# A 32-expert layer in a two-block transformer kernel: experts in a computed order, a fourth weight place, bias sums inside the first slots

## What is computed

```python
logits = xt @ w_router + b_router                       # 512 x 32
top_vals, top_idx = lax.top_k(logits, 4)
gates = softmax(top_vals)
# every token goes to its 4 experts; for the rows xb of expert e:
gt = minimum(xb @ w_gate[e] + b_gate[e], 7)
up = clip(xb @ w_up[e] + b_up[e], -7, 7)
hid = gt * sigmoid(1.702 * gt) * (up + 1)
y = hid @ w_down[e] + b_down[e]
out = sum over the 4 choices of gate * y
x = layer_norm(ALPHA * h + out)
```

## Time and profile before

| | us |
|---|---|
| median of 3 runs | 2679.3 (2677.22 to 2679.68) |
| profiled execution | 2679.23 |
| its span | 2677.5 |
| TensorE matmul busy | 2380.6 (89%) |
| VectorE busy | 644.8 (24%) |
| ScalarE busy | 321.6 (12%) |
| DMA | 570.64 MB, mean 213 GB/s |

### The profile page before, as it was taken

The page is one execution under the profiler, slowest core; times in us unless marked ns, Lnnn a source line. Parts: engine busy times, 40 slices in busy tenths (PEclk is TensorE's granted clock), DMA queues, the critical chain, the costliest instruction groups (busy, mean ns, idle before and its releaser), DMA issues. The chain is left out here.

```text
span 2677.5 us, 25039 instructions
## 1 busy us (share of the span) xinstructions
PE 2380.6 (89%) x9489; PEld 1036.1 (39%) x9490; DVE 644.8 (24%) x1376; ACT 321.6 (12%) x653; POOL 306.4 (11%) x295
## 2 busy tenths in 40 slices
PE   6999999798999999898978878999999889998980
PEld 4445666443444444344453223333333223332320
DVE  1322556441000000413343111111111111111116
ACT  1211222300000000003110000111111001110100
POOL 1003111002110010201210000000000000000005
PEclk7999999799999999899967988999999889998995
DMA  7353222202512122220045999889968999989954
GB/s 301 157 188 80 79 87 95 87 0 96 230 63 82 44 94 79 77 100 1 8 186 202 418 420 407 307 297 361 361 233 339 420 420 368 372 316 421 356 200 173
DMA packets 189003, 570.64 MB, mean 213 GB/s; under 512 B 12279, under 2 KB 47276, under 8 KB 186892
## 3 DMA queue, kind: packets, MB, share of 16 engines
q1 hardware_dynamic: 172832, 528.15, 51.4%
q0 software_dynamic: 6432, 21.66, 2.2%
q10 hardware_dynamic: 9676, 19.99, 2.2%
HBM read 545.57 MB, written 24.18 MB: 213 GB/s over the span
## 5 line engine op out<-in xcount | busy, mean ns | idle before, releaser
L1997 PE MATMUL banks<-expert_ring,slot_xT_gate 128*64 128x512 f32 x1440 | 370.6, 662 | 102.4 <-DMA expert_ring<-in_w_gate_dram 101.8
L1997 PE MATMUL banks<-expert_ring,hiddenT 128*64 128x512 f32 x1440 | 318.4, 595 | 2.1 <-DVE hiddenT L2067 2.1
L1997 PE MATMUL banks<-expert_ring,slot_xT_up 128*64 128x512 f32 x1440 | 318.9, 595 | 0.0
L1997 PEld LDWEIGHTS banks<-expert_ring,slot_xT_gate 128*64 128x64 f32 x1440 | 110.8, 152 | 324.0 <-issue 306.8
L1168 PE MATMUL banks<-hT,weight_ring 128*128 128x512 f32 x512 | 223.5, 597 | 6.7 <-PEq L2186 4.6
L1186 PE MATMUL banks<-weight_ring,hidden_T 128*128 128x512 f32 x512 | 220.7, 593 | 1.6 <-PE banks L1168 1.2
L1997 PEld LDWEIGHTS banks<-expert_ring,hiddenT 128*64 128x64 f32 x1440 | 103.6, 138 | 208.8 <-issue 206.4
L1997 PEld LDWEIGHTS banks<-expert_ring,slot_xT_up 128*64 128x64 f32 x1440 | 99.4, 137 | 187.4 <-issue 187.4
L2060 DVE TENSOR_TENSOR up_act_T<-banks,expert_bias_T 128x512 f32<-128x512 f32 x45 | 31.1, 692 | 503.9 <-PE banks L1961 503.9
L1168 PEld LDWEIGHTS banks<-hT,weight_ring 128*128 128x128 f32 x512 | 97.4, 192 | 132.4 <-issue 132.4
L1186 PEld LDWEIGHTS banks<-weight_ring,hidden_T 128*128 128x128 f32 x512 | 96.9, 190 | 125.3 <-issue 125.3
(11 more groups left out here) (372 smaller groups left out, 2190.4 us busy)
## 6 DMA issues: line engine op xcount, KB each, us to landing
expert_ring<-in_w_gate_dram SPq DMA_DIRECT2D x128, 1024.0 KB, 12.3
expert_ring<-in_w_up_dram SPq DMA_DIRECT2D x128, 1024.0 KB, 17.7
expert_ring<-in_w_down_dram SPq DMA_DIRECT2D x128, 1024.0 KB, 8.7
weight_ring<-in_w_ada_dram SPq DMA_DIRECT2D x12, 2048.0 KB, 11.3
weight_ring<-in_w_in_dram SPq DMA_DIRECT2D x8, 2048.0 KB, 14.7
weight_ring<-in_w_ff_in_dram SPq DMA_DIRECT2D x8, 2048.0 KB, 8.5
weight_ring<-in_w_ff_out_dram SPq DMA_DIRECT2D x8, 2048.0 KB, 7.8
weight_ring<-in_w_in_dram SPq DMA_DIRECT2D x24, 512.0 KB, 6.6
```

The costliest lines, as they stand in the source:

```text
L1997: x = nc.tensor.matmul(ps[h * CAP:(h + 1) * CAP, bank, :], lhs[:, k % 4, (k // 4) * CAP:(k // 4 + 1) * CAP], X.ring[:, m, k, h * HALF:(h + ...
```

## The change

- **An order of the experts.** The place of an expert is computed on the chip. Its key is 32 times its slots minus its number; experts 0 and 1 get the two lowest keys (0 and -1), so their ranks are 30 and 31. `place` lists the rank that stands at each place: 30, 31, then 0, 10, 20, 1, 11, 21, ... 9, 19, 29. So experts 0 and 1 come first, then one of each third of the ranking by turns. `M` is the one-hot matrix of expert and place. Running sums over the places are made by comparisons and by TensorE products with rows of ones (`hop`), which also spread them over the 128 partitions. `end_slot` and `slot_need` are now by place; `order` gives the expert of each place; the bias rows are turned by `M`, so that bias columns stand by place; `slot_source` is 3 x 8192 where a slot is the first of its expert, else 0.
- **A fourth place.** `expert_ring` has four places. The gate matrix of the next expert is loaded to place 3. In every slot ScalarE copies four parts of 128x2048 onto place 0 for the slot after (`move_gate`), from place 3 where that slot begins a new expert and from place 0 itself where not. TensorE's gate product waits for `moved[c]` instead of `landed[0][c]`. SyncE issues, for each place p: the gate matrix of place p+1 (once `moved[c]` has reached the first slot of p), the up and the down matrix of place p. Both take the expert number from a register. The gate matrix of expert 1 is prefetched in the route stage.
- **One-hot rows.** The sixteen pairs are made in two halves of eight, each with three wide operations.
- **Bias sums.** `bias_sum(t)` for t = 0 and 1 stands in slot 0 (ahead of the turn of the gate product, and behind the up product), for t = 2 and 3 in slot 1; VectorE's additions likewise. They use banks 6 and 7 alone.

```diff
+FIXED = 2
...
+            nc.gpsimd.iota(place_i[:, 0:FIXED], pattern=[[1, FIXED]], base=E - FIXED, channel_multiplier=0)\
+                .then_inc(q["iota_ok"], 1)
+            nc.gpsimd.iota(place_i[:, FIXED:], pattern=[[1, 10], [10, 3]], base=0, channel_multiplier=0)\
+                .then_inc(q["iota_ok"], 1)
...
+            one = G.ones[0:E, :]
+            pe.wait_ge(place_ok, 1)
+            nc.tensor.matmul(ps[:, 6, 0:E], one, diag[:], start=True, stop=True).then_inc(hop, 1)
+            pe.wait_ge(tab_ok, 1)
+            nc.tensor.matmul(ps[:, 7, 0:2 * E], one, tab[:].rearrange("p a e -> p (a e)"), start=True, stop=True)
+            nc.tensor.matmul(ps[0:E, 7, 2 * E:2 * E + 1], tab[:, 0, :], G.ones[0:E, 0:1], start=True, stop=True)\
+                .then_inc(hop, 1)
+            pe.wait_ge(before_ok, 1)
+            nc.tensor.matmul(ps[:, 6, 2 * E:3 * E], one, before[:], start=True, stop=True).then_inc(hop, 1)
+            pe.wait_ge(Z_ok, 1)
+            nc.tensor.matmul(ps[:, 7, 4 * E:4 * E + LIST], one, Z[:], start=True, stop=True).then_inc(hop, 1)
...
-                    x = nc.tensor.transpose(ps[:, 4, (m * KB + k) * E:(m * KB + k + 1) * E], b_rows[:, m, at:at + P],
-                                            G.ident[0:E, 0:E])
+                    x = nc.tensor.matmul(ps[:, 4, (m * KB + k) * E:(m * KB + k + 1) * E], b_rows[:, m, at:at + P], M[:],
+                                         start=True, stop=True)
...
             for c in range(TK):
-                pe.wait_ge(q["hot_ok"], c + 1)
-                nc.tensor.matmul(ps[:, 3, 0:LIST], colhot[:, c % 2, :], slothot[:, c % 2, :], start=(c == 0),
-                                 stop=(c == TK - 1)).then_inc(q["hot_used"], 1)
+                pe.wait_ge(q["hot_ok"], c // 8 + 1)
+                x = nc.tensor.matmul(ps[:, 3, 0:LIST], colhot[:, c, :], slothot[:, c, :], start=(c == 0), stop=(c == TK - 1))
+            x.then_inc(q["list_done"], 1)
...
-            a, s = 0, 1
-            while s < E:
-                nc.vector.tensor_copy(nb[:, 1 - a, 0:s], nb[:, a, 0:s])
-                step(nc.vector.tensor_tensor(nb[:, 1 - a, s:], nb[:, a, s:], nb[:, a, 0:E - s], ALU.add))
...
-            nc.vector.tensor_scalar(G.last_slot[:], upto[:, E - 1:E], -1.0, None, ALU.add)
-            nc.vector.tensor_copy(G.end_slot[:], upto)
-
-            step(nc.vector.tensor_tensor(cmp_[:], bc_mid(upto, LIST), bc_last(iota[:, 0:LIST], E), ALU.is_le))
-            step(nc.vector.tensor_reduce(sef[:], cmp_[:], AX_X, ALU.add))
-            step(nc.vector.tensor_scalar(sef[:], sef[:], float(E - 1), None, ALU.min))
-            nc.vector.tensor_scalar(G.slot_bias[:], sef[:], 2.0 * KB, None, ALU.mult)
-            nc.vector.tensor_scalar(G.slot_need[:], sef[:], 16.0, 16.0, ALU.mult, ALU.add)
...
+            eye, numbers, own = G.ident[0:E, 0:E], iota[0:E, 0:E], tok[0:E, 0:1]
+            nc.vector.scalar_tensor_tensor(out=key[:], in0=nrow[0:E, :], scalar=float(E), in1=numbers, op0=ALU.mult,
+                                           op1=ALU.subtract)
+            step(nc.vector.tensor_tensor(sq[:], nrow[0:E, :], eye, ALU.mult))
+            nc.vector.tensor_scalar(key[:, 0:FIXED], numbers[:, 0:FIXED], -1.0, None, ALU.mult)
+            step(nc.vector.tensor_reduce(n_col[:], sq[:], AX_X, ALU.add))
+            step(nc.vector.tensor_tensor(sq[:], key[:], eye, ALU.mult))
+            step(nc.vector.tensor_reduce(k_col[:], sq[:], AX_X, ALU.add))
+            step(nc.vector.tensor_scalar(sq[:], key[:], k_col[:, 0:1], None, ALU.is_gt))
+            step(nc.vector.tensor_reduce(r_col[:], sq[:], AX_X, ALU.add))
+            step(nc.vector.tensor_scalar(M[:], place[:], r_col[:, 0:1], None, ALU.is_equal))
+            step(nc.vector.tensor_tensor(sq[:], M[:], numbers, ALU.mult))
+            step(nc.vector.tensor_reduce(p_col[:], sq[:], AX_X, ALU.add))
+            nc.vector.tensor_scalar(diag[:], eye, p_col[:, 0:1], None, ALU.mult).then_inc(place_ok, 1)
+
+            nc.vector.tensor_scalar(tab[:, 0, :], numbers, p_col[:, 0:1], n_col[:, 0:1], ALU.is_ge, ALU.mult)
+            nc.vector.tensor_scalar(tab[:, 1, :], M[:], own, None, ALU.mult).then_inc(tab_ok, 1)
...
+            dve.wait_ge(hop, 1)
+            nc.vector.tensor_scalar(before[:], ps[0:E, 6, 0:E], p_col[:, 0:1], n_col[:, 0:1], ALU.is_gt, ALU.mult)\
+                .then_inc(before_ok, 1)
...
+            dve.wait_ge(hop, 2)
+            nc.vector.tensor_copy(upto[:], ps[:, 7, 0:2 * E].rearrange("p (a e) -> p a e", e=E))
+            step(nc.vector.tensor_copy(u_col[:], ps[0:E, 7, 2 * E:2 * E + 1]))
+            nc.vector.tensor_scalar(Z[:], iota[0:E, 0:LIST], u_col[:, 0:1], None, ALU.is_ge).then_inc(Z_ok, 1)
...
-            for c in range(TK):
-                if c >= 2:
-                    dve.wait_ge(q["hot_used"], c - 1)
-                nc.vector.tensor_scalar(colhot[:, c % 2, :], rank[:], col[:, c:c + 1], None, ALU.is_equal)
-                nc.vector.tensor_scalar(slothot[:, c % 2, :], iota[:, 0:LIST], sl[:, c:c + 1],
-                                        tok2[:, c // TOP_K:c // TOP_K + 1], ALU.is_equal, ALU.mult).then_inc(q["hot_ok"], 1)
+            for h in range(2):
+                at = slice(8 * h, 8 * h + 8)
+                nc.vector.tensor_tensor(colhot[:, at, :], bc_mid(rank[:], 8), bc_last(col[:, at], P), ALU.is_equal)
+                step(nc.vector.tensor_tensor(slothot[:, at, :], bc_mid(iota[:, 0:LIST], 8), bc_last(sl[:, at], LIST),
+                                             ALU.is_equal))
+                x = slothot[:, at, :].rearrange("p (t k) s -> p t (k s)", k=TOP_K)
+                nc.vector.tensor_tensor(x, x, bc_last(tok2[:, 2 * h:2 * h + 2], TOP_K * LIST), ALU.mult)\
+                    .then_inc(q["hot_ok"], 1)
...
+            nc.vector.tensor_scalar(G.last_slot[:], upto[:, 0, E - 1:E], -1.0, None, ALU.add)
+            nc.vector.tensor_copy(G.end_slot[:], upto[:, 0, :])
+            nc.vector.tensor_copy(G.order[:], upto[:, 1, :])
+            dve.wait_ge(hop, 4)
+            step(nc.vector.tensor_scalar(sef[:], ps[:, 7, 4 * E:4 * E + LIST], float(E - 1), None, ALU.min))
+            nc.vector.tensor_scalar(G.slot_bias[:], sef[:], 2.0 * KB, None, ALU.mult)
+            nc.vector.tensor_scalar(G.slot_need[:], sef[:], 16.0, 16.0, ALU.mult, ALU.add)
+            step(nc.vector.tensor_tensor(new[:, 1:], sef[:, 1:], sef[:, 0:LIST - 1], ALU.subtract))
+            nc.vector.tensor_scalar(G.slot_source[:], new[:], float(3 * KB * D), None, ALU.mult)
...
-        self.ring = ctx.enter_context(nc.sbuf_tensor("expert_ring", [P, self.MATS, KB, D], F32))
+        self.ring = ctx.enter_context(nc.sbuf_tensor("expert_ring", [P, self.MATS + 1, KB, D], F32))
...
-        src = w[e, k0 * P:(k0 + nk) * P, :].rearrange("(k p) n -> p k n", p=P)
-        sp.dma_start(self.ring[:, m, k0:k0 + nk, :], src).then_inc(self.landed[m][c], 16)
+        src = w[bass.ds(e, 1), k0 * P:(k0 + nk) * P, :].rearrange("a (k p) n -> p (a k) n", p=P)
+        sp.dma_start(self.ring[:, m if place is None else place, k0:k0 + nk, :], src).then_inc(self.landed[m][c], 16)
...
+        for c in range(self.PARTS):
+            sp.wait_ge(self.landed[0][c], 16)
+            self.load(sp, 0, c, 1, self.MATS)
...
-            for e in range(1, EXPERTS):
-
-                end = sp.value_load(G.end_slot[0:1, e - 1:e], min_val=e, max_val=MAX_SLOTS)
-                for m in range(X.MATS):
+            for p in range(1, EXPERTS):
+                end = sp.value_load(G.end_slot[0:1, p - 1:p], min_val=p, max_val=MAX_SLOTS)
+                e = sp.value_load(G.order[0:1, p:p + 1], min_val=0, max_val=EXPERTS - 1)
+                if p + 1 < EXPERTS:
+                    following = sp.value_load(G.order[0:1, p + 1:p + 2], min_val=0, max_val=EXPERTS - 1)
+                    for c in range(PARTS):
+                        sp.wait_ge(moved[c], end)
+                        X.load(sp, 0, c, following, X.MATS)
+                for m in range(1, X.MATS):
                     for c in range(PARTS):
                         sp.wait_ge(used[m][c], end)
                         X.load(sp, m, c, e)
...
+            def move_gate(i):
+                at = G.slot_source[0:1, i:i + 1] if isinstance(i, int) else G.slot_source[0:1, bass.ds(i, 1)]
+                source = act.value_load(at, min_val=0, max_val=3 * KB * D)
+                landed = need(act, i)
+                flat_ring = X.ring[:].rearrange("p m k n -> p (m k n)")
+                size = KB * D // PARTS
+                for c in range(PARTS):
+                    act.wait_ge(X.landed[0][c], landed)
+                    nc.scalar.copy(flat_ring[:, c * size:(c + 1) * size], flat_ring[:, bass.ds(source + c * size, size)])\
+                        .then_inc(moved[c], 1)
...
                 gate_copy(i)
                 x_for_gate(i + 1)
+                move_gate(i + 1)
...
+            def bias_sum(t):
+                if t:
+                    pe.wait_ge(q["bias_added"], t)
```

(26 more changed lines are left out.)

91 lines of the change are left out of this document (47 added, 44 removed).

## The result

The changed kernel takes 2639.2 us (median of 4 runs, 2637.9 to 2643.1) against 2679.5 for the kernel before: a ratio of 0.985, 95% interval 0.983 to 0.987. It is 40 us faster; 71 were forecast, and the time lies inside the range of 2575 to 2645, 6 us from its upper end, and 31 us above the predicted 2608. The profiled execution spans 2636.4 us.

The account below looks back on a forecast made before the run. Expert stage bound by TensorE and weight loads nearly level, some 140 us above TensorE's need. Slot 2 at 1483.5 + 43 x 22.51 + 70 waits + 12.2 tail = 2533.6 against 2605.2, -71: 2608 us; range 2575 to 2645.

Parts of the forecast that it names:

- The wait moves to the up product, seven long ones: Expert stage: TensorE's wait for the gate product vanishes; about 7 long up-product waits near 6 us, first near place 11.
- The release at t + 12.1, landing at t + 17.0: Long expert's second slot, starting at t: next gate load issued at t + 12.1, its first part landing at t + 17.0.
- Copies 1.91 us, in cover: ScalarE, every slot: four copies of 1.91 us, 7.6 in all, costing nothing while a copy stays under some 3 us.
- 4c + 9: Rival that ScalarE becomes the bound (6%): shortest slot in us at c us a copy; loses from c = 4.1.
- A part each 2.50 us at 420 GB/s: Weight loads of the expert stage: after the first, a 1 MB part lands every 2.50 us, at 420 GB/s.
- loads slower: Rival (12%): new traffic at place 3 makes parts slower than 2.5 us; at 2.6 some +30 us, 2638.
- The 2586 us by the fit: Whole-kernel estimate if a DMA takes 2.0 us plus its bytes at 436 GB/s, making a part 2.4 us.
- Short waits of 1.2, and 1.7 for the clock: Each late group: 1.2 us wait at the second short expert's last up part; 1.7 lost to half clock after the long wait.
- The clock rival: Rival (12%): nine short waits of 1.2 us each bring 7 us at half rate, costing 3 each: +27, 2635.
- The start: First slots: gate product starts near 1428 instead of 1437.3, but low clock and bias sums leave slot 2 at 1483.5.
- The route stage: Stage ahead of the experts: cheaper comparisons and one-hot rows make it 2 to 5 us earlier, taken as 3.
- The signs: Trace marks to check: among them slot periods of 22.5 in 38 of 44, late groups at 400 GB/s over 99 to 100 us.

Follow-up runs that it names:

- copy_twice: The changed kernel padded by 128 bytes ahead of the ring, with ScalarE copying every part of the gate matrix twice; 2673.2 us.
- align: The changed kernel with 128 bytes of unused padding a partition ahead of the ring, which then starts at a multiple of 256; 2619.6 us.
- bias_front: The changed kernel padded by 128 bytes ahead of the ring, with the four bias sums back ahead of slot 0; 2627.5 us.
- before_256: The kernel before with 256 bytes of padding ahead of the ring, which then starts at another multiple of 256; 2683.2 us.
- before_mis: The kernel before with 128 bytes of padding ahead of the ring, which then starts 128 past a multiple of 256; 2692.0 us.

## Why the prediction came out as it did

Its direction, and the mechanism of its sum, were right: the order and the fourth place cut the waits, and what is left stands at the up product. The gain was 40 us of the forecast 71, since two terms of the sum were too small: the time of a part, and the short waits. That the time still fell inside the range is in part luck, since an error of 8 us at the start went the other way. The author's own range of 2596 to 2622 was missed. Point by point:

- *The wait moves to the up product, seven long ones.* Right: seven of 6.1 to 6.4 us, the first at place 11, forecast 6.4.
- *The release at t + 12.1, landing at t + 17.0.* Right: with t = 2068.03 the load is issued at 2079.82, t + 11.8, and lands 5.0 later at t + 16.8.
- *Copies 1.91 us, in cover.* Right for the size, 1.895. "Cost nothing while a copy stays under some 3 us" looked at the wrong limit: the first copy stands in the release chain at any length. At 3.8 us, where 4c + 9 gives 24.2 us a slot and no loss before c = 4.1, copy_twice lost over 50 us, most of it at the release. The prediction had named this ("sooner since the loads start later too") and given it no price.
- *A part each 2.50 us at 420 GB/s.* **The first term that was mis-sized.** It took the rate of before for a property of the loads, while it was also one of the ring's address: 2.49 in align, 2.56 in the changed kernel. The prediction had the 29th part, the first up part of the next long expert, at t + 90.7; it landed at 2162.02, t + 94.0. The rival "loads slower" gave a time nearly right (2638) for a cause that align refutes, and with 2.6 a part: that was luck, since most of the missing time lies in the next point. The two buffers ahead of the ring stand in the changed kernel, but no row of before could show that their 384 bytes matter. Worth 15 us of the loss, 20 us of the medians. The 2586 us by the fit of the Trainium skill, DMA: Bandwidth & Descriptors (Anatomy of one DMA), was further off; the page states that fit for DMAs that GpSimd issues, and these loads are issued by SyncE.
- *Short waits of 1.2, and 1.7 for the clock.* **The second, and the larger in the loss.** The sum counted one late part at each place. Loads that land 2.5 us or more apart hold back, at every part, a product that uses one in 1.8 or 1.9. Ten places cost 41.3 us (forecast 7 x 1.2 + 4 = 12.4), 32.1 even with the ring aligned: slot 2, the first slots of the long experts at places 5 and 8, and seven second shorts. The sum had the three early ones at other places, 4, 7 and 10. The first slots of the seven longs cost 66.4 (forecast 7 x 8.1 = 56.7), 9.5 each: the wait of 6.3, 4.98 - 3.65 = 1.3 for 16 matmuls that began at the low clock, 0.8 of waits for parts, and some 1.0 that these rows don't place. The rows of tokens, in and out, also took more than was allowed: in align the 19 parts behind the first took 51.2 to 52.7 us, 3.9 to 5.3 above 19 x 2.49, where 2.5 stood in the sum.
- *The clock rival.* Refuted for the short waits: in 2121:2149, with four waits of 0.5 to 1.1 us, the granted clock is 1.00. For the long ones the low clock begins in the pause (0.50 in 2054:2057, with TensorE idle since 2051.8) and is over in 2061:2067. The oscillation that the Trainium skill names under TensorE: Matmul & The Clock Gate (second HAM failure mode) for small idles between groups doesn't show in these waits.
- *The start.* "So the nine microseconds won go mostly on low clock" was wrong, and in the other direction: slot 2 was forecast at 1483.5 and came at 1475.4, 8.1 us earlier. The gate product of slot 0 took 1437.49 - 1426.81 = 10.7 us, not 16, since the clock rose inside it (0.50 in 1430:1432, 1.00 in 1434:1438); and bias_front shows that what counts at this point is the release of the loads.
- *The route stage.* `slot_tokens` is ready at 1417.9 instead of 1419.7: 1.8 us, forecast 3.
- *The signs.* Of the 44 slot periods 25 are 22.5 us, where 38 were named; the sum itself had more late places than six. A late group takes 103.6 to 104.3 us at 383 GB/s, where 99 to 100 at 400 were named.

The account: forecast 2608, plus 9.7 for the longs (66.4 - 56.7), plus 28.9 for the ten places (41.3 - 12.4), minus 8.1 for the start, is 2638.5; measured 2639.2. Of the 38.6 us of larger waits align gives back 15.2; the other 23 are in how the waits were counted.

## What to carry to other kernels

Before comparing two versions of a kernel, compare where their large buffers start: a few small buffers allocated ahead of a ring of weights can cost a third of what the change brings, and a pad of 128 bytes gives it back. Where an engine waits for loads that come in parts, count the wait for every part against the time in which one is used, not for the first or the last alone. A lightly loaded engine that releases a load is on the path at that one moment: cost its operations by what they hold back, not by its busy share.

## What the runs showed of the hardware

- The start of the destination rows within 256 bytes of a partition goes with the pace of 1 MB loads: 2.49 us a part and 420 GB/s at a multiple of 256 (three addresses: before, before_256, align), 2.56 us and 410 GB/s at 128 past one (two addresses: before_mis, after), with and without the change. Other places within 256 bytes were not tried.
- ScalarE copies 128x2048 within SBUF in 1.90 us while the DMA engines write to the same buffer, and its copies don't slow the loads: 421 GB/s in 1937:1966 of align, with ScalarE busy 10 of 29 us.
- Four pauses of TensorE of 0.5 to 1.1 us within 9 us left its clock at 1.00 (2121:2149 of after); in a pause of 6.3 us it fell to 0.50 (2054:2057).
